# Two transformer blocks on one core: the second mixer's queries are normalised inside the attention, not before it

## The reference, cut to what matters

```python
pl, pc = u_lat @ w, u_ctx @ w          # w: 1024 x (1024 + 256 + 256)
ql = rms_norm(ql, swa_q_gain)          # over the 64 of a head
kl, kc = rms_norm(kl, swa_k_gain), rms_norm(kc, swa_k_gain)
ql, kl = apply_axial_rope(ql, cos, sin), apply_axial_rope(kl, cos, sin)
s_loc = where(valid, ql . kl * 64 ** -0.5, NEG_INF)
s = concatenate([s_loc, ql . kc * 64 ** -0.5, s_sink])
y_lat = (softmax(s)[..., :-1] @ [vl, vc]) @ swa_wo
```

## Time and profile before

| | us |
|---|---|
| median of 3 runs | 1704.48 |
| lowest and highest | 1704.2, 1707.45 |
| the profiled execution's own time | 1704.0 |
| its span, first to last instruction | 1701.9 |
| TensorE busy | 1607.5 (94%) |
| VectorE busy | 1303.2 (77%) |
| ScalarE busy | 870.8 (51%) |
| mean granted clock of TensorE | 0.979 |

### The profile page before, as it was taken

One profiled execution on the slowest core, in us unless ns is written; L12 is line 12 of the kernel. 1 busy time (PEld: TensorE's weight loads), 2 busy tenths in 40 slices (PEclk: granted clock), 3 DMA queues, 4 the chain that ended last, 5 costly groups with the idle time before them and its releaser, 6 DMA issues.

```text
span 1701.9 us, 32714 instructions
## 1 busy us (share of the span) xinstructions
PE 1607.5 (94%) x11872; PEld 1424.8 (84%) x11872; DVE 1303.2 (77%) x2245; ACT 870.8 (51%) x1505; POOL 104.6 (6%) x174
## 2 busy tenths in 40 slices
PE   6999899899999999788989999889999999899999
PEld 4778666688888888675789999789999998699999
DVE  5899897788767867678678787777887686578874
ACT  4664386344213333466665555355555586555552
POOL 0001030000000023120000212000000000000000
PEclk9999999999999999898999999999999999999999
DMA  9246651345567855341156667735555644055554
GB/s 370 88 138 229 217 149 51 123 134 187 198 198 232 266 184 157 125 125 31 63 182 209 208 215 268 304 107 178 177 181 186 197 161 150 13 167 181 182 198 136
DMA packets 80828, 292.22 MB, mean 172 GB/s; under 512 B 10432, under 2 KB 12224, under 8 KB 78800
## 3 DMA queue, kind: packets, MB, share of 16 engines
q1 hardware_dynamic: 69552, 249.03, 44.2%
q0 software_dynamic: 11168, 41.74, 7.6%
HBM read 270.74 MB, written 18.68 MB: 170 GB/s over the span
## 4 chain that ended last, share of the span: by engine, by line
PE 75%; DVE 16%; issue 4%; ACT 3%; DMA 2%; ACTq 0%; DVEq 0%; SPq 0%; POOLq 0%
PE bank L730 22%; PE bank L731 22%; PE bank L732 22%; DVE w_lo L1577 2%; PE bank L914 2%; PE bank L925 2%; PE bank L940 1%; DVE bank L1589 1%; DVE ada_raw L1590 1%; DVE stat L2126 1%; DMA raw<-weights 1%; DVE prob L2138 1%; DVE qk L1772 1%; DMA ada_raw<-ada_w 1%; PE bank L818 1%
## 5 line engine op out<-in xcount | busy, mean ns | idle before, releaser
L730 PE MATMUL bank<-u_hi,w_hi 128*128 128x256 f32 (+1 forms) x1936 | 617.1, 319 | 30.8 <-DVE u_lo L1952 18.7
L731 PE MATMUL bank<-u_lo,w_hi 128*128 128x256 f32 (+1 forms) x1936 | 602.5, 311 | 0.0
L732 PE MATMUL bank<-u_hi,w_lo 128*128 128x256 f32 (+1 forms) x1936 | 602.3, 311 | 0.0
L1577 DVE TENSOR_TENSOR w_lo<-raw,w_hi 128x1024 fp32r<-128x1024 f32 x372 | 452.1, 1222 | 143.9 <-ACT w_hi L1144 131.7
L1144 ACT ACTIVATE w_hi<-raw 128x1024 fp32r<-128x1024 f32 x360 | 375.6, 1050 | 172.8 <-PE bank L732 141.8
L730 PEld LDWEIGHTS bank<-u_hi,w_hi 128*128 128x128 f32 x1936 | 374.0, 193 | 58.5 <-issue 35.8
L731 PEld LDWEIGHTS bank<-u_lo,w_hi 128*128 128x128 f32 x1936 | 374.2, 193 | 22.3 <-issue 3.8
L732 PEld LDWEIGHTS bank<-u_hi,w_lo 128*128 128x128 f32 x1936 | 374.2, 193 | 18.7
L730 PE MATMUL bank<-hid_hi,w_hi 128*128 128x512 f32 (+1 forms) x512 | 174.0, 340 | 0.0
L732 PE MATMUL bank<-hid_hi,w_lo 128*128 128x512 f32 (+1 forms) x512 | 172.1, 336 | 0.0
L731 PE MATMUL bank<-hid_lo,w_hi 128*128 128x512 f32 (+1 forms) x512 | 172.1, 336 | 0.0
(11 more groups left out here) (317 smaller groups left out, 2259.1 us busy)
## 6 DMA issues: line engine op xcount, KB each, us to landing
raw<-weights SPq DMA_DIRECT2D x372, 512.0 KB, 3.4
ada_raw<-ada_w SPq DMA_DIRECT2D x80, 512.0 KB, 4.1
ada_first<-ada_w SPq DMA_DIRECT2D x16, 512.0 KB, 13.3
bias_sb<-bias_na POOLq DMA_DIRECT2D x16, 256.0 KB, 3.3
toep_dram<-zeros POOLq DMA_DIRECT2D x8, 512.0 KB, 8.9
bat_dram<-bat POOLq DMA_DIRECT2D x16, 256.0 KB, 4.4
ca_dram<-ca POOLq DMA_DIRECT2D x16, 256.0 KB, 3.4
...
```

The costliest lines, as they stand in the source:

```text
L730: pe.matmul(dst, wh, hi[:, kt, xs], start=first, stop=False)
L731: pe.matmul(dst, wh, lo[:, kt, xs], start=False, stop=False)
L732: return pe.matmul(dst, wl, hi[:, kt, xs], start=False, stop=final)
L1577: TT(w_lo[:, slot, :], raw[:, slot, :], w_hi[:, slot, :].bitcast(F32), ALU.subtract).then_inc(S["lo"], 1)
```

## The change

- **Queries unscaled.** q1 is a "plain" stage: ScalarE squares a tile and copies it to q1 times the gain; no root and no scaling. VectorE does no work on the tile but the rotation.
- **Head sums in two batches.** The squares of four tiles are kept. Two batches of four matmuls (query_sums), in q1's fifth tile and k1's first, gather the sums of all 16 heads in one bank, 32 rows a matmul, with two pick columns held in silu_pad (query_picks). ScalarE copies the bank, TensorE turns it (query_turn), so that a query's sum stands on the query's partition, and VectorE and ScalarE make q_neg, minus one over the norm, of 128 x 32 numbers (query_mean, query_root, query_norm).
- **Joined pass.** att_max multiplies by the column of q_neg where it multiplied by -1.
- **Exchange in six.** Query tiles go in pairs, the key tiles alone. Of the first key tile SP sends the upper half, from a place between two of wo1's loads. The rotations come in the order 0 to 5, 8, 6, 7, 9; the last stands in the attention.
- **Early first scores.** v1 uses banks 2 and 3 for both units. The scores of groups 0 and 1 stand in v1's second unit, behind its second and third slices; groups take bank pairs 0 and 3, results banks 2 and 3. VectorE's first joined pass and ScalarE's first exp move into v1's stage. The common waits ahead of the attention go, and each score waits for the rotations that it needs.
- stat and neg_sink have other places, the stages q1 on ScalarE and VectorE are written out without a loop.

```diff
 Stage("down0b", "RES", 8, units=2, tok=TOK, norm=True, gate=(0, 5)),
-Stage("q1", "QK", 8),
+Stage("q1", "QK", 8, plain=True),
 Stage("k1", "QK", 2, tok=TOK),
...
 HANDOVER = {"v0": (("qk0", ("a1", "d1")),), "down0a": (("up0a", ("a1",)),), "up0b": (("down0a", ("d1",)),),
-            "down0b": (("up0b", ("a1",)),), "k1": (("q1", ("a1", "d1")),),
-            "v1": (("k1", ("a1", "d1")), ("q1", ("a1", "d1"))), "down1a": (("up1a", ("a1",)),),
+            "down0b": (("up0b", ("a1",)),), "k1": (("q1", ("a1", "a3")),),
+            "v1": (("q1", ("a1", "a3")),), "down1a": (("up1a", ("a1",)),),
             "up1b": (("down1a", ("d1",)),), "down1b": (("up1b", ("a1",)),), "q2": (("k2", ("a1", "a3")),),
...
+TURNS = ((0, 1), (2, 3), (4, 5), (6, 7), (8,), (9,))
+TURN_OF = {m: n for n, tiles in enumerate(TURNS) for m in tiles}
+ROPE_ORDER = (0, 1, 2, 3, 4, 5, 8, 6, 7, 9)
+ROPE_PLACE = {m: n for n, m in enumerate(ROPE_ORDER)}
+def q_at(hp):
+    return hp % 4 * 4 + hp // 4 * 2
+def score_pair(g):
+    return g % 2 if g < 32 else (0, 3)[g % 2]
+def out_bank(g):
+    return psum[(6 if g < 32 else 2) + g // 2 % 2]
 MODS_NEEDED = {"mix0": 4, "mlp0": 10, "mix1": 16, "mlp1": 22}
+def value_bank(s, pair, b):
+    return TILE[2 + b] if s.name == "v1" else TILE[pair % 2 * 2 + b]
 VAL = {"v0": val0, "v1": val1, "v2": val2}
...
                 load_ada(a + 2)
+    continue
+if s.name == "wo1":
+    for g in range(s.unit0, s.unit0 + s.tiles):
+        load_unit(g, g % RING)
+        if g == s.unit0 + 3:
+            turn_first_keys()
     continue
...
         sum_tile(*sums[t // 3])
+    if s.name == "q1" and i * body + jj == 4 and t == 2:
+        query_sums(0)
+    if s.name == "k1" and jj == 0 and t == 2:
+        query_sums(1)
+    if s.name == "k1" and jj == 0 and t == 5:
+        query_turn()
 mm.then_inc(S["unit"], 1)
...
     mm = pe.matmul(dst, hi[:, kt, xs], wl, start=False, stop=final, skip_group_check=True)
-if t == 1:
+if s.name == "v1" and jj == 1 and t in (1, 2):
+    att_scores(ATT1, t - 1, 32)
+if t == (0 if s.name == "v1" else 1):
     for owed in sums_inside(s, i * body + jj):
...
     pe.matmul(SUM_BANKS[b2][:, 0:s.tok], C("block"), sq[:, b2, 0:s.tok], start=True, stop=True).then_inc(S["p2"], 1)
+def query_sums(b):
+    if b == 0:
+        pe.wait_ge(pick_made, 1)
+    pe.wait_ge(S["a1"], value("a1", ST["q1"], 4 * b + 4))
+    for n in range(4):
+        mm = pe.matmul(psum[6][32 * n:32 * n + 32, 0:SEQ], silu_pad[:, b, :], sq[:, n // 2, n % 2 * SEQ:(n % 2 + 1) * SEQ],
+                       start=(b == 0), stop=(b == 1), skip_group_check=True)
+    mm.then_inc(S["p2"], 4)
+def query_turn():
+    pe.wait_ge(q_copied, 1)
+    for qt in range(2):
+        mm = pe.transpose(psum[7][:, qt * P:(qt + 1) * P], q_cols[:, qt * P:(qt + 1) * P], C("ident"))
+    mm.then_inc(q_turned, 1)
...
 g = m + base
-if g >= 2:
+if base and m == 0:
+    stage_end(pe, ST["k1"], ("a1", "d1"))
+if base and m == 1:
+    pe.wait_ge(q_mean, 2)
+if base and m % 2 == 0:
+    pe.wait_ge(rope_d, 1 + (max(ROPE_PLACE[n] for n in (m // 2, 8)) if m < 8 else ROPE_PLACE[9]))
+if g >= 2 and not (base and m < 2):
...
 gemm("k1")
-gemm("v1"); drained("v1"); drained("q1"); drained("k1")
-pe.wait_ge(rope_d, 10)
+gemm("v1")
 attention(ATT1, 32)
...
+if s.name == "k1":
+    if jj == 0:
+        query_copy()
+    else:
+        qk_root(s, i, jj - 1, body)
 act.wait_ge(S["unit"], n_done)
+if s.more.get("plain"):
+    if j >= 4:
+        act.wait_ge(S["p2"], value("p2", s, 4))
+    A(sq[:, j % 4 // 2, j % 2 * SEQ:(j % 2 + 1) * SEQ], bank[:, 0:s.tok], ACT.Square).then_inc(S["a1"], 1)
+    A(q1[:, j, :], bank[:, 0:s.tok], ACT.Copy, scale=VC(QK_GAIN[s.name][0], j)).then_inc(S["a3"], 1)
+    return
 act.wait_ge(S["p2"], value("p2", s, j - 1))
...
         late_root(s, j - 1)
+elif s.name == "k1":
+    if jj == 0:
+        query_root()
 elif jj:
...
 elif s.kind == "V":
+    if s.name == "v1" and jj == 1:
+        att_exp(ATT1, 0, 32)
     if jj % 2:
...
+def query_copy():
+    act.wait_ge(S["p2"], value("p2", ST["q1"], 8))
+    A(q_cols[:, :], psum[6][:, 0:SEQ], ACT.Copy).then_inc(q_copied, 1)
+def query_root():
+    act.wait_ge(q_mean, 2)
+    root(q_y[:, :, :], q_v[:, :, :]).then_inc(q_root, 1)
 def late_root(s, j):
...
        rsn[:, 0:SEQ].rearrange("p (c s) -> p s c", s=CH), ALU.mult).then_inc(S["d1"], 1)
+elif s.more.get("plain"):
+    rope({5: (0,), 6: (1,), 7: (2,)}.get(j, ()))
 elif s.kind == "QK":
+    if s.name == "k1":
+        if jj == 0:
+            rope((3,))
+            query_mean()
+            rope((4,))
+        else:
+            rope((5,))
     dve.wait_ge(S["a1"], value("a1", s, j + 1))
     dve.tensor_copy(dcol(QK_DST[s.name], j, all_), bank[:, all_]).then_inc(S["d1"], 1)
-    if jj:
+    if s.name == "k1":
+        if jj == 0:
+            query_norm()
+            qk_scale(s, i, 0, body)
+    elif jj:
         qk_scale(s, i, jj - 1, body)
...
+def query_picks():
+    dve.wait_ge(row_made, 2)
+    link(dve.tensor_copy(silu_pad[:, 0, 0:2], C("block")[:, HD - 1:HD + 1]))
+    link(dve.memset(silu_pad[:, 1, 0:2], 0.0))
+    dve.tensor_copy(silu_pad[:, 1, 2:4], C("block")[:, HD - 1:HD + 1]).then_inc(pick_made, 1)
+def query_mean():
+    dve.wait_ge(q_turned, 1)
+    for qt in range(2):
+        sums = psum[7][:, qt * P:(qt + 1) * P].rearrange("p (g r) -> p g r", r=32)[:, :, 0:4]
+        TS(q_v[:, qt, :].rearrange("p (g r) -> p g r", r=4), sums, -0.5 * INV_HD, -0.5 * EPS,
+           ALU.mult, ALU.add).then_inc(q_mean, 1)
+def query_norm():
+    dve.wait_ge(q_mean, 2)
+    dve.wait_ge(q_root, 1)
+    v, y = q_v[:, :, :], q_y[:, :, :]
+    link(TT(v, v, y, ALU.mult))
+    link(STT(v, v, -1.0, y, ALU.mult, ALU.mult))
+    link(STT(q_neg[:, :, :], v, -1.5, y, ALU.add, ALU.mult))
+    link(TS(neg_sink[:, :], VC("sink", 0, n=HEADS), -1.0, None, ALU.mult))
 def rope(tiles):
...
 dst = q1[:, m, :] if m < 8 else k1[:, m - 8, 0:SEQ]
-dve.wait_ge(rope_in[m // 4], 16 * 8)
-if m >= 2:
-    dve.wait_ge(rope_d, m - 1)
-link(TT(prob[:, m % 2, 0:SEQ], turned[:, m, :], C("sin"), ALU.mult))
+dve.wait_ge(rope_in[TURN_OF[m]], 16 * (4 if m == 8 else 8))
+if m == 8:
+    dve.wait_ge(rope_in_sp, 16 * 4)
+n = ROPE_PLACE[m]
+if n >= 2:
+    dve.wait_ge(rope_d, n - 1)
+link(TT(rope_sin[:, n % 2, :], turned[:, m, :], C("sin"), ALU.mult))
 link(TT(dst, dst, C("cos"), ALU.mult))
-TT(dst, dst, prob[:, m % 2, 0:SEQ], ALU.add).then_inc(rope_d, 1)
+TT(dst, dst, rope_sin[:, n % 2, :], ALU.add).then_inc(rope_d, 1)
...
     lower(s.unit0 + jj + 3, i, per)
-if s.name == "k1":
-    rope((range(0, 2), range(2, 4))[jj])
-if s.name == "v1":
-    rope((range(4, 6), range(6, 10))[jj])
+if s.name == "v1" and jj == 0:
+    rope((8, 6))
+    qk_scale(ST["k1"], 0, 1, 2)
+    rope((7,))
+if s.name == "v1" and jj == 1:
+    att_max(ATT1, 0, 32)
 if s.name == "qk0":
...
 for a in range(2):
-    dve.tensor_tensor_reduce(both[:, a, :], both[:, a, :], window, -1.0, neg_sink[:, 2 * hp + a:2 * hp + a + 1],
+    dve.tensor_tensor_reduce(both[:, a, :], both[:, a, :], window,
+                             q_neg[:, qt, q_at(hp) + a:q_at(hp) + a + 1], neg_sink[:, 2 * hp + a:2 * hp + a + 1],
                              ALU.add, ALU.min, stat[:, 0, b, a:a + 1]).then_inc(att_m, 1)
...
 norm(2, "mix1")
-stage("q1")
+query_picks()
 dve.wait_ge(late_in, 16)
-stage("k1"); stage("v1")
-link(TS(neg_sink[:, :], VC("sink", 0, n=HEADS), -1.0, None, ALU.mult))
+stage("q1"); stage("k1"); stage("v1")
 attention(ATT1, 32)
...
 pool.dma_start(rot[:, :, :, :], rot_dram).then_inc(rot_in, 16)
-for n, (name, done) in enumerate((("q1", 4), ("q1", 8), ("k1", 2))):
-    pool.wait_ge(S["d2"], value("d2", ST[name], done))
+for n, tiles in enumerate(TURNS):
+    made, name = ("a3", "q1") if n < 4 else ("d2", "k1")
+    pool.wait_ge(S[made], value(made, ST[name], tiles[-1] % 8 + 1))
     if n == 0:
...
         p1 = p0 + 16 if p0 % 32 == 0 else p0 - 16
-        src_ = q1[p1:p1 + 16, 4 * n:4 * n + 4, :] if n < 2 else k1[p1:p1 + 16, :, 0:SEQ]
-        pool.dma_start(turned[p0:p0 + 16, 4 * n:4 * n + (4 if n < 2 else 2), :], src_).then_inc(rope_in[n], 16)
+        m0, m1 = tiles[0], tiles[-1] + 1
+        if n == 4 and p0 >= P // 2:
+            break
+        src_ = q1[p1:p1 + 16, m0:m1, :] if n < 4 else k1[p1:p1 + 16, m0 - 8:m1 - 8, 0:SEQ]
+        pool.dma_start(turned[p0:p0 + 16, m0:m1, :], src_).then_inc(rope_in[n], 16)
 stage_end(pool, ST["wo1"], ("unit",))
```

More of the change, by code:

```diff
@@ L677, in sums_inside @@
                     return ((ST[prev], ST[prev].tiles - 1),) if prev else ()
-                if s.kind != "QK" or s.name in KT_FIRST and j < lead(s):
+                if s.kind != "QK" or s.more.get("plain") or s.name in KT_FIRST and j < lead(s):
                     return ()
@@ L913, in att_scores @@
                     q_ap, k_ap, _ = heads[a]
-                    pe.matmul(psum[2 * (g % 2) + a][:, 0:keys], q_ap, k_ap, start=True, stop=True).then_inc(att_s, 1)
```

(22 more changed lines are left out.)

40 lines of the change are left out of this document (26 added, 14 removed).

## The result

| | before | changed |
|---|---|---|
| median of the runs beside each other, us | 1705.41 (4 runs) | 1693.52 (4 runs) |
| lowest and highest | 1704.2, 1707.45 | 1689.85, 1694.75 |
| the profiled execution, its span | 1704.0, 1701.9 | 1694.75, 1692.9 |

The account below looks back on a forecast made before the run. TensorE, busy 94% of the span, was taken as the bound, with waits and slow clock to remove. Terms -14.5, -0.4, +1.2, +0.1 sum to -13.6 us: 1690.4, or 1690.9 as median, range 1687 to 1693.5 (chance 0.72).

Parts of the forecast that it names:

- q1: Second layer's query stage: both waits for ScalarE's square and the slow stretch go; it ends 7.0 us earlier.
- batch of sums: In q1's tile 4: four head sums issued together, plus the change back to products, cost 1.14 us.
- weight part: In q1: three small VectorE operations for pick columns stand ahead of tile 3's weight part, costing 0.45 us without cover.
- k1: Key stage after q1: second batch of sums and two transposes lengthen it from 12.3 to 13.4 us.
- v1 and the keys' way: From v1's start through exchange and rotations: first joined pass at 762.1 instead of 776.56, 14.5 us earlier.
- landing of 4.0 us: Key tile 0's exchange in v1: slower landing gives 755.2 instead of 753.8, still before VectorE reaches that rotation.
- Start of the attention: First groups: gain of 1.1 us at full clock, loss of about 1 if it falls; 0.4 gain taken.
- rival B: Attention's first groups: slow clock stays after 2.3 us idle, 1.0 plus up to 2 us lost, 1694 us; chance 0.09.
- Rotation in the loop: Attention loop: key tile 1's rotation, 1.25 us on VectorE, stands between two joined passes; 1.2 us lost.
- column factor: Joined pass in the loop: factor from a tensor column costs 0 to 0.06 us an instruction, 0.1 us in all.
- rival C: Attention's joined passes slow by up to 0.7 us each, 1711 us; sign: pass of 0.8 us or more; chance 0.03.
- Sum: Whole kernel: -14.5 - 0.4 + 1.2 + 0.1 = -13.6 us against the profiled execution.

Follow-up runs that it names:

- fewroots: Kernel before, q1's root logarithm and exponential taken of one column instead of 256, queries' norm left out: 1702.83 us, ratio 0.9991.
- roots: Changed kernel with four extra ScalarE passes on each query tile in q1, nothing left out: 1695.7 us, ratio 0.9946 to the kernel before.
- onequeue: Changed kernel with all eight pieces of key tile 0's exchange issued by GpSimd: 1692.02 us, ratio 0.9932 to the kernel before.
- again: Changed kernel once more, nothing edited: 1691.59 us in six runs, ratio 0.9915 to the kernel before.
- noearly: Changed kernel with no score group inside v1; first scores follow v1's last product: 1691.79 us, ratio 0.9927 to the kernel before.
- banks: Kernel before with only v1's tiles moved to banks 2 and 3: 1706.28 us, ratio 1.0005.
- norot9: Changed kernel with the last rotation left out, second key tile unrotated: 1689.69 us, ratio 0.9908 to the kernel before.
- const: Changed kernel with constant -1.0 as the joined pass's factor, queries' norm left out: 1689.09 us, ratio 0.9911 to the kernel before.

## Why the prediction was right

- **q1** was to give 7.0 us by k1's start; it gave 7.4 (35.98 to 28.58 us behind q1's first product). The cause is confirmed both ways, by fewroots (3.2 us for 0.44 us less per tile) and roots (6.0 us lost). What makes up the rest of the 7.4, single sums and VectorE's copies and scalings, has no run of its own. The batch of sums was put a little too dear: 1.14 us forecast, 0.95 measured. (The last product before it starts at 723.46 and the second one after it at 724.65: 1.19 us, where two of the other matmuls would be 0.24.) The weight part that was to cost 0.45 us cost 0.30.
- **k1** was to last 13.4 us and lasted 12.9 (734.97 to 747.84): its batch cost 0.76 us by the same reckoning, and the transposes 0.22 in place of 0.44.
- **v1 and the keys' way** held step by step. v1 starts 8.7 us earlier against q1 (1.72 of it the wait of before), and from there to the first joined pass it is 14.31 us where it was 21.24. Those 6.9 us were followed in rows only: no run takes out the exchange in six or the rotation that was moved into the loop. VectorE waited for ScalarE's split where I had put it, at 754.00 against 753.8. I dated from a q1 at 705.16, and this one began at 706.39, so the chain came 1.0 us better than forecast, as q1 and k1 had. The first joined pass at 762.15 against 762.1 hides that. The exchange landed in time, and onequeue shows how close: 0.23 us too late when one queue issues all eight. Two readings of the prediction were off without bearing on the sum: with a landing of 4.0 us (755.2) VectorE would have been at the rotation already, at 755.0; and between the six rotations of before stands a weight part of 1.22 us. 16 KB landed in 1.6 to 1.8 us here and in 2.3 in onequeue, 32 KB in 3.4. The Trainium skill (DMA: Bandwidth & Descriptors, "Anatomy of one DMA") gives a GpSimd transfer a fixed 2.0 us or so, and adds the bytes at 436 GB/s: an estimate of 2.1 us for 32 KB. That is near the 16 KB pieces and too little for the 32 KB ones.
- **Start of the attention**: forecast a gain of 0.4, between a full clock's 1.1 and a loss of 1. Measured, what is left of the attention's 1.57 us without the rotation and the column is a gain of 0.39 (1.57 - 1.08 - 0.88; by again 1.40 - 0.91 - 0.88). The clock fell (0.50 in 767 to 769 us), as in rival B, and roots prices that at 0.58 to 0.75 us, less than B's up to 3.
- **Rotation in the loop**: 1.2 forecast, 0.90 to 1.08 measured.
- **The column factor** is the term that was wrong in size: 0.1 us forecast, 0.88 measured. The step that failed is "0 to 0.12 against 0.11 of slack". The 0.06 us a pass was right. But slack holds only in the even part; at the first groups, beside the rotation and at the end VectorE is what TensorE waits for, and each pass there pays in full. Besides, it took the last slack of the even part. The sign given for rival C, a joined pass of 0.8 us or more, appeared (0.81) without C: the passes of a pair start 0.73 us apart where it was 0.67.
- The attention as a whole: forecast 0.9 us longer (-0.4 + 1.2 + 0.1), measured 1.57. With the rotation at 1.08, the column at 0.88 and the clock at 0.75, the remainder is 1.57 - 2.71 = -1.1 us (-1.0 by again), near the 1.1 us that the prediction gave its start at full clock. It is a remainder and not a measurement of its own.
- **Sum** of the stretch: -13.6 forecast, -14.07 measured. The gain was put 1.1 too low on the way and 0.7 too high in the attention. That the total came close owes something to luck: those two errors cancel in part. The two parts that looked like its second half, early scores and free banks, gave nothing by themselves (noearly, banks).

Open is what decided the clock behind the wait of 2.21 us. It fell in changed, again and norot9 (2.21 us), in onequeue (2.54) and in noearly (2.78), and stayed at 1.00 in roots (2.21) and const (2.09). No run was made that changes only that.
